# Sample attention of a decoder step: keys turned by VectorE, scores on small TensorE tiles, value products ahead of the filler

## The chip, the cores and the metric

The kernel runs on one core of a Trainium2 chip. The metric is the device time of one execution in microseconds (us); of the kernel before, three runs gave 3669.8, 3672.9 and 3675.2 us, median 3672.9.

## The reference, cut to what matters

One inference step of a hybrid decoder layer, for a prompt group (1024 tokens) and a sample group (8 sequences of 8 tokens). The change concerns the sample group's forgetting attention over a paged cache:

```python
k_all = jnp.concatenate([past_k, fk], axis=1)        # 4096 cached tokens (32 pages of 128) + 8 new
v_all = jnp.concatenate([past_v, fv], axis=1)
c_all = lax.cumsum(lf_all, axis=1)                   # log forget gates
s = jnp.einsum('bqhd,bkhd->bhqk', qi, k) * scale     # 8 heads of 64
s = s + ci[..., None] - ckT                          # bias c_t - c_s
p = jax.nn.softmax(s, axis=-1)
o = jnp.einsum('bhqk,bkhd->bqhd', p, v)
```

Everything is float32. Each page holds 128 tokens x 512 numbers (8 heads x 64), 256 KB for keys and as much for values; 256 pages are read of each.

## The kernel before, in words

The program is a row of phases with a barrier of all engines between them. Two of them are touched.

`phase_sample_bias` gathers the pages' forget gates, turns them on TensorE, adds them up over pages on VectorE (`tot`), and makes each page's bias with 16 pairs of matmuls, `own` (L2207) and `behind` (L2208), two halves of 8 pairs, whose stationary operand is 128 columns wide (16 pages x 8 heads). ScalarE copies each half out of PSUM (L2220), SyncE stores it to `bias_past` in DRAM (L2167). GpSimd also lays the queries out in `qz`.

`phase_sample` walks 8 sequences in 9 steps each: step 0 the 8 new tokens, steps 1 to 8 a quad of 4 pages. It goes on with the third gate of the merge, `w_fox_o` and the gate's weights, as filler: per sequence one block j of 128 channels. Every engine has its order written out in a loop over k = 0 to 75. TensorE's, in iteration k:

- `turn(u, 0)`, `turn(u, 1)` (L2488): 4 transposes of 128x128 for each of the first two pages of the quad that step k+1 needs, into PSUM (`ktp`, two buffers); ScalarE's `place` (L2629) copies each to `kt`.
- `turn_probs(k-1)` (L2501): 2 transposes of the exponentials, copied by VectorE's `place` (L2699) to `pt`.
- `fill(k)`: one piece of filler. Of a block's 9 pieces, 0, 1, 3, 4 are 12 gate matmuls of 512 columns (L2564), 2 and 5 are the output product (L2575), 6 is 24 gate matmuls of 64 columns; 7 and 8 are empty.
- `turn(u, 2)`, `turn(u, 3)`.
- `scores(k)` (L2516): 8 float32 products, `qz` stationary (128 rows x 32 columns, one of four column groups), 256 keys each. A float32 product is two instructions.
- `products(k-1)` (L2533): 8 products, `pt` stationary (32 columns), 256 value columns each.

Score rows of the same head and query stand in two column groups, one for even and one for odd pages, and are joined at the sequence's end (`swap_stats`, `pair_weights`, `finish`). VectorE adds the bias and takes the running minimum (`top`, L2717), ScalarE takes exponentials (`exps`, L2640), VectorE accumulates (L2728). `stp`, `ptp` and `ov` have two buffers.

SyncE issues all page loads: 4 key pages as their slots are turned, then 4 value pages once `valued` frees theirs (L2415, L2418); there is room for two quads of each. GpSimd issues bias loads (L2437) and the filler's weights (L2443, L2459) and splits these in high and low parts.

Of the kernel before, what the change touches and what calls it, by code (L numbers as in the profile page):

```python
# [13 lines left out]
F32 = mybir.dt.float32  # L14
# [42 lines left out]
def shape_tables():  # L57
# [19 lines left out]
    def dec(steps):  # L77
# [22 lines left out]
    set_of, row_of = i // 32, i % 32  # L100
    new_mask = np.tile(new.transpose(2, 1, 0), (P // LSEQ, 1, 1))
    new_mask[set_of % 2 == 1] = NEG
    swap = (i[None, :] == (i ^ 32)[:, None])
    comb = ((set_of // 2 * 32 + row_of)[:, None] == j[None, :])
# [4 lines left out]
        "new_mask": new_mask, "swap": swap, "comb": comb,  # L109
# [154 lines left out]
def phase_load(g):  # L264
# [3 lines left out]
    with ExitStack() as ctx:  # L268
# [8 lines left out]
        n_const = 8  # L277
        xs = io["x_sample"].rearrange("b t d -> (b t) d")
        with nc.Block() as block:
            @block.sync  # L280
            def _(sp):
# [21 lines left out]
                for e in range(2):  # L303
                    half = g.pages[:].rearrange("o (b n e) -> o b n e", b=NSEQ, e=2)[:, :, :, e]
                    sp.dma_start(half, io["page_table"][:, e * (NPG // 2):(e + 1) * (NPG // 2)].unsqueeze(0),
                                 allow_slow_non_contiguous=True).then_inc(consts, 16)
# [1828 lines left out]
def phase_sample_bias(g, qz, bias_n, bias_past):  # L2135
# [5 lines left out]
    with ExitStack() as ctx:  # L2141
# [5 lines left out]
        mask, lfx = g.sb(ctx, "d_mask", [P, NSEQ, TS]), g.sb(ctx, "d_lfx", [TS, 2, 2, 4, LSEQ])  # L2147
        out = g.sb(ctx, "d_out", [P, 2 * NSEQ, P])
        t = [g.ps(ctx, f"d_t{j}", [P, H_F, P]) for j in range(2)]
        sums = g.ps(ctx, "d_sums", [P, NSEQ, P])  # L2150
# [3 lines left out]
        expanded, cn_ok, qz_ok = g.sem("d_expanded"), g.sem("d_cn_ok"), g.sem("d_qz_ok")  # L2154
        indexed = g.sem("d_indexed")
        with nc.Block() as block:
            @block.sync
            def _(sp):
# [5 lines left out]
                for x in range(2):  # L2164
                    sp.wait_ge(read, x + 1)
                    for c in range(x * NSEQ, (x + 1) * NSEQ):
                        sp.dma_start(bias_past[c].rearrange("h g t -> g h t"), out[:, c, :]).then_inc(stored, 16)  # L2167
# [3 lines left out]
            def _(pool):  # L2171
# [6 lines left out]
                nc.gpsimd.memset(qz[:], 0.0).then_inc(qz_ok, 1)  # L2178
                pool.wait_ge(qz_ok, 1)
                pool.wait_ge(paged, 32)  # L2180
                for i in range(2):
                    q = g.br[:, 8 + i:12:2, TP:T].rearrange("p a (b q) -> p b a q", q=LSEQ)
                    for s in range(2):
                        at = 2 * LSEQ * i + LSEQ * s
                        nc.gpsimd.tensor_copy(qz[HALVES[s], :, i:PAIRS:2, at:at + LSEQ], q[HALVES[s]])

            @block.tensor
            def _(pe):
# [8 lines left out]
                nc.tensor.matmul(cn[:], lfx[:].rearrange("p a e s q -> p (a e s q)"), upto[:], start=True, stop=True)\  # L2197
                    .then_inc(cn_ok, 1)
                pe.wait_ge(copied, 2)
                pe.wait_ge(steps, 6)  # L2200
                for c in range(2 * NSEQ):
# [3 lines left out]
                    own = lft[:, b, x * HG:(x + 1) * HG, :].rearrange("p g h -> p (g h)")  # L2205
                    behind = tot[1][:, b, x * HG + 1:(x + 1) * HG + 1, :].rearrange("p g h -> p (g h)")
                    nc.tensor.matmul(sums[:, c % NSEQ, :], own, after[:], start=True, stop=False)  # L2207
                    mm = nc.tensor.matmul(sums[:, c % NSEQ, :], behind, g.ones[:], start=False, stop=True)  # L2208
# [4 lines left out]
            def _(act):  # L2213
                for j in range(2):
                    act.wait_ge(turned, j + 1)
                    nc.scalar.copy(lft[:, j * 4:j * 4 + 4].rearrange("p b g h -> p h (b g)"), t[j][:])\
                        .then_inc(copied, 1)
                for x in range(2):
                    act.wait_ge(summed, x + 1)
                    nc.scalar.copy(out[:, x * NSEQ:(x + 1) * NSEQ, :], sums[:]).then_inc(read, 1)  # L2220

            @block.vector
            def _(dve):
                chain = Chain(steps)
                nc.vector.memset(lfx[:], 0.0).then_inc(expanded, 1)
                for s in range(2):
                    nc.vector.memset(tot[s][:, :, NPG, :], 0.0)
                dve.wait_ge(expanded, 1)
                nc.vector.tensor_copy(lfx[:, :, 0], g.lfn[0:TS, NCH, :].rearrange("p (a s) -> p a s", s=4).unsqueeze(3)
                                      .broadcast_to([TS, 2, 4, LSEQ])).then_inc(expanded, 1)  # L2230
# [13 lines left out]
                assert now == 1 and chain.n == 6  # L2244
# [5 lines left out]
def phase_mix_two(g, mix):  # L2250
# [3 lines left out]
    with ExitStack() as ctx:  # L2254
# [72 lines left out]
        w.n = [b[0] + KD, b[1] + KD]  # L2327


def phase_sample(g, qz, bias_n, bias_past, mix):  # L2330

# [687 lines left out]
```

## Time and profile before

| | us |
|---|---|
| median of 3 runs | 3672.9 |
| profiled execution | 3673.46 |
| its span, first to last instruction | 3671.6 |
| PE busy / DVE / ACT / POOL | 3314.7 / 888.4 / 625.5 / 794.6 |
[...]

The span is the trace's; the execution's own time lies 1.9 us above it. PE is TensorE's matmuls, PEld its weight loads, DVE is VectorE, ACT ScalarE, POOL GpSimd, SP SyncE. Busy shares are means over very different stages, so one reads the two touched stages by themselves. They lie, in the trace, at about 1716 to 1768 us (bias) and 2091 to 2616 us (sample attention).

### The profile page before, as it was taken

The page shows a single profiled execution, that of the slowest core. Times are in us where ns is not written, and L with a number is a line of the kernel's source. Part 1 is how long each engine was busy: PE and PEld are TensorE (multiplying, and loading weights), DVE is VectorE, ACT ScalarE, POOL GpSimd, SP SyncE. Part 2 cuts the span into 40 slices and gives each one's busy share as a digit, 9 for nine tenths or more (in the row PEclk, how much of TensorE's full clock was granted, in tenths as well). Part 3 has the DMA queues.
Part 4 walks back from the last instruction along what each step waited for, and adds up shares of the span by engine and source line. Part 5 has one row for each costly group of instructions (what it writes and reads, how often), then busy time and mean ns, then how long its engine had stood idle before and what let it go on. Part 6 is the DMA issues. An engine that isn't in the chain of part 4 may idle for free. (4 is left out here: it accounts for less than half of the span.)

```text
span 3671.6 us, 56105 instructions
## 1 busy us (share of the span) xinstructions
PE 3314.7 (90%) x21121; PEld 2999.5 (82%) x21121; DVE 888.4 (24%) x1581; ACT 625.5 (17%) x1163; POOL 794.6 (22%) x696
## 2 busy tenths in 40 slices
PE   5999999997988898786799899999796999999996
PEld 5999999996887798554688666666686999999995
DVE  2111111114206211555101022222314111111114
ACT  3000000002101100344000144434203000000003
POOL 0232222323120131022111111111021223233220
PEclk8999999998997899899899999999798999999998
DMA  5111111111110112210211299999311111111111
GB/s 141 35 51 40 42 49 34 49 49 29 29 44 22 41 40 67 91 48 17 52 43 43 60 297 307 300 305 303 121 29 29 34 46 50 33 51 43 37 37 55
DMA packets 328667, 293.12 MB, mean 80 GB/s; under 512 B 33640, under 2 KB 249064, under 8 KB 328048
## 3 DMA queue, kind: packets, MB, share of 16 engines
q1 hardware_dynamic: 317136, 275.93, 24.3%
q0 software_dynamic: 11424, 15.76, 1.6%
q8 instruction: 68, 1.11, 0.1%
q14 instruction: 39, 0.32, 0.0%
HBM read 279.34 MB, written 12.26 MB: 79 GB/s over the span
## 5 line engine op out<-in xcount | busy, mean ns | idle before, releaser
L207 PE MATMUL f_acc<-x_hi,w_hi_last 128*128 128x364 f32 x1056 | 233.5, 329 | 27.5 <-SPq L489 27.5
L165 POOL CAST w_hi_first<-w_raw_first 128x1024 fp32r<-128x1024 f32 (+1 forms) x96 | 82.9, 863 | 738.4 <-issue 301.3
L207 PE MATMUL f_acc<-x_hi,w_hi_first 128*128 128x364 f32 x1056 | 233.5, 329 | 6.9 <-SPq L489 6.9
L207 PE MATMUL f_acc<-x_lo,w_hi_last 128*128 128x364 f32 x1056 | 234.0, 330 | 0.0
L207 PE MATMUL f_acc<-x_hi,w_lo_last 128*128 128x364 f32 x1056 | 234.0, 330 | 0.0
L207 PE MATMUL f_acc<-x_hi,w_lo_first 128*128 128x364 f32 x1056 | 233.9, 330 | 0.0
L207 PE MATMUL f_acc<-x_lo,w_hi_first 128*128 128x364 f32 x1056 | 233.7, 329 | 0.0
L207 PEld LDWEIGHTS f_acc<-x_hi,w_hi_last 128*128 128x128 f32 x1056 | 184.0, 189 | 28.0 <-issue 28.0
L165 POOL CAST w_hi_last<-w_raw_last 128x1024 fp32r<-128x1024 f32 (+2 forms) x92 | 73.5, 799 | 614.2 <-PE f_acc L207 610.2
L596 DVE SCALAR_TENSOR_TENSOR br<-f_acc,br 128x1092 f32 x88 | 114.1, 1296 | 368.8 <-PE f_acc L207 368.8
L207 PEld LDWEIGHTS f_acc<-x_hi,w_hi_first 128*128 128x128 f32 x1056 | 184.0, 189 | 7.1 <-issue 7.1
L167 POOL TENSOR_TENSOR w_lo_first<-w_raw_first,w_hi_first 128x1024 fp32r<-128x1024 f32 (+1 forms) x96 | 185.5, 1933 | 7.7
L207 PEld LDWEIGHTS f_acc<-x_hi,w_lo_last 128*128 128x128 f32 x1056 | 184.4, 189 | 0.0
L207 PEld LDWEIGHTS f_acc<-x_hi,w_lo_first 128*128 128x128 f32 x1056 | 184.2, 189 | 0.0
L207 PEld LDWEIGHTS f_acc<-x_lo,w_hi_last 128*128 128x128 f32 x1056 | 183.8, 189 | 0.0
L207 PEld LDWEIGHTS f_acc<-x_lo,w_hi_first 128*128 128x128 f32 x1056 | 183.7, 189 | 0.0
L2488 PEld LDWEIGHTS d_ktp<-ident_sb,br 128*128 128x128 f32 x1024 | 115.7, 143 | 83.1 <-DMA br<-cache_fox_k 45.5
L2488 PE MATMUL d_ktp<-ident_sb,br 128*128 128x128 f32 x1024 | 145.3, 283 | 34.8 <-DMA br<-cache_fox_k 32.7
L167 POOL TENSOR_TENSOR w_lo_last<-w_raw_last,w_hi_last 128x1024 fp32r<-128x1024 f32 (+2 forms) x92 | 162.9, 1771 | 7.4
L583 DVE TENSOR_TENSOR br<-br,f_acc 128x1092 f32<-128x1092 f32 x22 | 28.4, 1293 | 452.1 <-PE f_acc L207 452.1
L583 DVE TENSOR_TENSOR hid<-silu,f_acc 128x1092 f32<-128x1092 f32 x22 | 28.4, 1292 | 452.2 <-PE f_acc L207 452.2
L207 PE MATMUL f_acc<-h_hi,w_hi_last 128*128 128x364 f32 x528 | 118.0, 332 | 2.6 <-DVE h_lo L587 2.6
(399 smaller groups left out, 6321.8 us busy)
## 6 DMA issues: line engine op xcount, KB each, us to landing
br<-cache_fox_k SPq DMA_DIRECT2D x256, 256.0 KB, 5.6
br<-cache_fox_v SPq DMA_DIRECT2D x256, 256.0 KB, 6.5
w_raw_first<-w_ffn_gate SPq DMA_DIRECT2D x22, 512.0 KB, 3.8
w_raw_first<-w_ffn_up SPq DMA_DIRECT2D x22, 512.0 KB, 3.8
w_raw_last<-w_ffn_gate SPq DMA_DIRECT2D x22, 512.0 KB, 3.8
w_raw_last<-w_ffn_up SPq DMA_DIRECT2D x22, 512.0 KB, 3.8
w_raw_first<-w_ffn_down SPq DMA_DIRECT2D x40, 256.0 KB, 2.9
w_raw_last<-w_ffn_down SPq DMA_DIRECT2D x40, 256.0 KB, 2.8
```

Of the source, the lines that this page charges most:

```text
L165: self.nc.gpsimd.tensor_copy(hi, raw).then_inc(self.high[s], 1)
L167: self.nc.gpsimd.tensor_tensor(lo, raw, hi.bitcast(F32), ALU.subtract).then_inc(self.low[s], 1)
L207: mm = self.nc.tensor.matmul(out[:, b, 0:width], w[s][:, k, :], x[:, k, b * width:(b + 1) * width], start=(k == 0 and first), stop=(k == k ...
L583: nc.vector.tensor_tensor(blocks_of(hid), blocks_of(silu), acc[1][:, :, 0:TB], ALU.mult).then_inc(free[1], 1)
L596: nc.vector.scalar_tensor_tensor(blocks_of(row), acc[s][:, :, 0:TB], 0.5, blocks_of(row), ALU.mult, ALU.add).then_inc(free[s], 1)
L2488: mm = nc.tensor.transpose(ktp[n % 2][:, c, :], k_in[:, s, c * P:(c + 1) * P], g.ident[:])
```

## The change

- **Keys.** TensorE's 16 transposes per quad and ScalarE's 4 copies go. VectorE turns the quad in two instructions of 128 x 1024 numbers, which transpose each 32x32 block by itself (`turn`), after `top(k)` and ahead of `accumulate(k-1)`.
- **Scores.** 64 float32 products per quad (128 instructions), each on one 32x32 tile of the array: 32 rows, 32 stationary columns, 128 moving columns. Four row groups write to four PSUM banks. `stp` has one buffer. ScalarE replicates the queries for this (`queries`, two small copies per step).
- **Probabilities.** 512 per row and step instead of 256: 4 transposes, copied by ScalarE (`place`); one buffer each of `ptp`, `pt`, `ov`. All pages of a head share a row, so the joining at the end goes.
- **Products.** 16 of 128 value columns instead of 8 of 256.
- **Order of TensorE:** scores(k), turn_probs(k-1), products(k-1), turn_out, fill(k).
- **Filler.** Three blocks of 364 columns instead of 512, 512 and 64; all 9 pieces are filled.
- **Bias phase.** The 16 pairs of matmuls become 64 pairs with a stationary operand 32 columns wide (4 pages x 8 heads), and VectorE and ScalarE make 4 copies each to lay out `behind` and `own`. The layout of `qz` leaves this phase. Its 16 stores have 32 rows of 2 KB each.
- **Page table.** One load instead of two at the program's start.

```diff
@@ phase_sample_bias, TensorE @@
-                    nc.tensor.matmul(sums[:, c % NSEQ, :], own, after[:], start=True, stop=False)
-                    mm = nc.tensor.matmul(sums[:, c % NSEQ, :], behind, g.ones[:], start=False, stop=True)
+                    group, pages = slice(ROWS * (c % 4), ROWS * (c % 4 + 1)), slice(x * QUAD, (x + 1) * QUAD)
+                    for n in range(QUAD):
+                        at = by_token[group, c // 4 % 2, n]
+                        nc.tensor.matmul(at, own[:, b, n, pages, :]..., after[:], start=True, stop=False, ...)
+                        mm = nc.tensor.matmul(at, behind[:, b, n, pages, :]..., g.ones[:], start=False, stop=True, ...)
@@ phase_sample_bias, VectorE @@
+                for n in range(QUAD):
+                    nc.vector.tensor_copy(behind[:, :, n], tot[1][:, :, n + 1:NPG + 1:QUAD]).then_inc(behind_ok, 1)
@@ phase_sample, SyncE @@
+                        sp.wait_ge(k_turned, c * 4 + (2 * half + 2))
                         for s in range(half * QUAD, (half + 1) * QUAD):
-                            sp.wait_ge(k_turned, c * CH + (s + 1))
-                            sp.dma_start(k_in[:, s, :], keys[ahead[s]]...).then_inc(k_ok[s], 16)
+                            load_key(s, ahead[s])
@@ phase_sample, TensorE: scores @@
+                    pe.wait_ge(k_turned, 2 * (u + 1))
+                    for s in range(2):
+                        for h in range(2):
+                            for x in range(4):
+                                rows = slice(ROWS * x, ROWS * (x + 1))
+                                for c in range(PAIRS):
+                                    block = 4 * c + 2 * s + h
+                                    q = q_rep[e][rows, block * QW - s * LSEQ:block * QW - s * LSEQ + ROWS]
+                                    mm = nc.tensor.matmul(out[ROWS * c:ROWS * (c + 1), x], q,
+                                                          kt[u % 2][rows, :, block * ROWS:(block + 1) * ROWS],
+                                                          start=(s == 0 and h == 0), stop=(s == 1 and h == 1), ...)
+                    mm.then_inc(scored, 1)
@@ phase_sample, TensorE: order of an iteration @@
                 for k in range(STEPS_ALL + 4):
-                    u = quad_after(k)
-                    if u is not None:
-                        turn(u, 0)
-                        turn(u, 1)
+                    if k < STEPS_ALL:
+                        scores(k)
                     if 0 < k <= STEPS_ALL:
                         turn_probs(k - 1)
...
-                    fill(k)
-                    if u is not None:
-                        turn(u, 2)
-                        turn(u, 3)
-                    if k < STEPS_ALL:
-                        scores(k)
                     if 0 < k <= STEPS_ALL:
                         products(k - 1)
+                    if k >= PIECES + 1 and (k - 1) % PIECES == 0:
+                        turn_out((k - 1) // PIECES - 1)
+                    fill(k)
@@ phase_sample, ScalarE: an iteration @@
+                    if 0 < k <= STEPS_ALL:
+                        place(k - 1)
                     gate_read(k)
+                    if k + PIECES < STEPS_ALL:
+                        queries(k // PIECES + 1, k % PIECES)
                     if k < STEPS_ALL:
                         exps(k)
@@ phase_sample, VectorE @@
+                def turn(u):
+                    for s in range(u % 2 * QUAD, (u % 2 + 1) * QUAD):
+                        dve.wait_ge(k_ok[s], 16 * (u // 2 + 1))
+                    if u >= 2:
+                        dve.wait_ge(scored, step_of(u - 2) + 1)
+                    for y in range(2):
+                        nc.vector.transpose(kt[u % 2][:, 2 * y:2 * y + 2, :], k_in[:, u % 2, 2 * y:2 * y + 2, :])\
+                            .then_inc(k_turned, 1)
```

## Rows read from the trace of the kernel before

**Rows 1.** Windows, sample stage: length, busy us of each engine, PEclk, DMA share, GB/s.
```profile
2100.00:2591.00 491.00, 459.88 (x4087) 314.84 (x4087) 133.31 (x406) 205.18 (x498) 79.36 (x111) 0.97 0.92 300
```
**Rows 2.** Groups of the sample stage: shape, count, busy us, mean ns, idle before.
```profile
L2488 PE MATMUL d_ktp<-ident_sb,br 128*128 128x128 f32 x1024 | 145.3, 283 | 34.8 <-DMA br<-cache_fox_k 32.7 <-ACT mem_kt L2629 1.0
...
L2629 ACT COPY d_kt<-d_ktp 128x512 f32<-128x512 f32 x128 | 69.9, 587 | 78.6 <-PE d_ktp L2488 77.4
...
L2575 PE MATMUL fx_out<-br,fx_wo 128*128 128x512 f32 x128 | 57.6, 592 | 0.0
...
L2717 DVE CUSTOM_DVE_ANT_0 d_ring<-d_stp,d_ring,d_nm 128x256 f32<-128x256 f32 x64 | 31.0, 484 | 181.7 <-PE d_stp L2516 181.7
...
L2666 ACT ACTIVATE br<-fx_gate,br 128x512 f32<-128x512 f32 x16 | 11.0, 688 | 43.6 <-PE fx_gate L2564 43.6
```
**Rows 3.** Timeline of one step with a gate piece: start, us, instruction, count.
```profile
2567.67 1.10 PE L2488 MATMUL d_ktp<-ident_sb,br 128*128 128x128 f32 x8
...
2568.61 0.38 PE L2501 MATMUL d_ptp<-ident_sb,d_ring 128*128 128x128 f32 x2
...
2569.03 0.43 DVE L2699 COPY d_pt<-d_ptp 128x256 f32<-128x256 f32 x1 [0.59 <-PE d_ptp L2501]
...
2571.62 1.04 PE L2488 MATMUL d_ktp<-ident_sb,br 128*128 128x128 f32 x8
...
2572.60 0.40 PE L2516 MATMUL d_stp<-mem_v,d_qz 128*32 128x256 f32 x1
2572.61 0.40 PE L2516 MATMUL d_stp<-mem_kt,d_qz 128*32 128x256 f32 x1
...
2573.48 1.05 PE L2533 MATMUL d_ov<-br,d_pt 128*32 128x256 f32 x16
...
2574.46 1.09 PE L2488 MATMUL d_ktp<-ident_sb,br 128*128 128x128 f32 x8
```
**Rows 4.** Waits in the sample stage: us in total, times, longest.
```profile
PEld d_ktp L2488 <- DMA br<-cache_fox_k: 45.5, 34, 12.9
...
PEld d_ov L2533 <- DMA br<-cache_fox_v: 12.9, 22, 1.7
```
**Rows 5.** Windows of 2 us in the sample stage.
```profile
2442.00:2444.00 2.00, 2.00 (x6) 0.90 (x5) 0.00 (x0) 0.00 (x0) 0.00 (x0) 1.00 1.05 402
...
2446.00:2448.00 2.00, 2.00 (x32) 1.33 (x25) 0.97 (x3) 0.98 (x4) 0.00 (x0) 1.00 0.33 119
...
2488.00:2490.00 2.00, 2.00 (x18) 1.56 (x17) 0.00 (x0) 0.36 (x1) 0.00 (x0) 1.00 1.07 257
```
**Rows 6.** Timeline of the bias phase's sums.
```profile
1748.10 0.77 PE L2207 MATMUL d_sums<-d_after,d_lft 128*128 128x128 f32 x2 [14.45 <-DVE d_tot L2241]
...
1754.44 1.01 ACT L2220 COPY d_out<-d_sums 128x1024 f32<-128x1024 f32 x1 [18.70 <-PE d_sums L2208]
...
1755.84 0.39 PE L2208 MATMUL d_sums<-ones_sb,d_tot 128*128 128x128 f32 x2
...
1758.96 0.39 PE L2208 MATMUL d_sums<-ones_sb,d_tot 128*128 128x128 f32 x2
1759.38 1.01 ACT L2220 COPY d_out<-d_sums 128x1024 f32<-128x1024 f32 x1 [3.93 <-PE d_sums L2208]
```
**Rows 7.** Windows, bias phase and the retention phase's sample part.
```profile
1155.00:1170.00 15.00, 13.47 (x56) 12.21 (x56) 7.27 (x24) 0.00 (x0) 0.00 (x0) 0.50 0.22 52
...
1750.00:1752.00 2.00, 2.00 (x11) 2.00 (x11) 0.00 (x0) 0.00 (x0) 0.00 (x0) 0.50 0.00 0
...
1756.00:1758.00 2.00, 2.00 (x20) 2.00 (x20) 0.00 (x0) 0.00 (x0) 0.00 (x0) 1.00 0.27 66
```
**Rows 8.** VectorE's groups of 1024 and 512 numbers from SBUF to SBUF.
```profile
L2238 DVE TENSOR_TENSOR d_tot<-d_tot 128x1024 f32<-128x1024 f32 x1 | 1.2, 1226 | 0.0
...
L2241 DVE COPY d_tot<-d_tot 128x512 f32<-128x512 f32 x1 | 0.4, 420 | 0.0
```
**Rows 9.** Windows, first feed-forward phase, all matmuls of 364 columns.
```profile
200.00:300.00 100.00, 100.00 (x601) 100.00 (x600) 14.57 (x10) 5.70 (x6) 31.19 (x22) 1.00 0.17 49
```

More of the change, by code:

```diff
@@ L302, in _ @@
                 sp.dma_start(g.b_forget[:], io["b_forget"].rearrange("(h o) -> h o", o=1)).then_inc(consts, 16)
[L303 to L306, printed above, removed]
+                sp.dma_start(g.pages[:], io["page_table"].rearrange("b n -> (b n)").unsqueeze(0)).then_inc(consts, 16)
                 sp.wait_ge(consts, 16 * n_const)
@@ L2217, in _ @@
                         .then_inc(copied, 1)
+                act.wait_ge(copied, 2)
+                for n in range(QUAD):
+                    nc.scalar.copy(own[:, :, n], lft[:, :, n:NPG:QUAD]).then_inc(own_ok, 1)
                 for x in range(2):
                     act.wait_ge(summed, x + 1)
-                    nc.scalar.copy(out[:, x * NSEQ:(x + 1) * NSEQ, :], sums[:]).then_inc(read, 1)
+                    nc.scalar.copy(out[:, x * 2:(x + 1) * 2, :], sums[:]).then_inc(read, 1)
             @block.vector
@@ L2467, in _ @@
-                weights(0)
+                for e in range(2):
+                    nc.gpsimd.memset(q_rep[e][:], 0.0).then_inc(zeroed, 1)
+                    nc.gpsimd.memset(qz[e][:], 0.0).then_inc(zeroed, 1)
                 bias(0)
-                split(0)
                 bias(1)
+                raw_half(0, 0)
+                out_weights(0)
+                split_half(0, 0)
+                raw_half(0, 1)
                 for b in range(NSEQ):
-                    more = b + 1 < NSEQ
-                    if more:
-                        bias(2 * b + 2)
-                        weights(b + 1)
-                        split(b + 1)
-                        bias(2 * b + 3)
+                    split_half(b, 1)
+                    bias(4 * b + 2)
+                    bias(4 * b + 3)
+                    if b + 1 < NSEQ:
+                        bias(4 * b + 4)
+                        raw_half(b + 1, 0)
+                        bias(4 * b + 5)
+                        out_weights(b + 1)
+                        split_half(b + 1, 0)
+                        raw_half(b + 1, 1)
@@ L2498, in turn_probs @@
                     else:
-                        half, m = divmod(b * (PIECES - 1) + v - 1, QUAD)
-                        for x in range(2):
-                            mm = nc.tensor.transpose(ptp[:, k % 2, x, :], ring[half % 2][:, m, x, :], g.ident[:])
+                        for y in range(QUAD):
+                            mm = nc.tensor.transpose(ptp[:, y, :], probs[:, y, :], g.ident[:])
                     mm.then_inc(pturned, 1)
@@ new lines, in scores @@
+                    if k > 0:
+                        pe.wait_ge(topped, k)
+                    if k >= PIECES + 2 and v == 2:
+                        pe.wait_ge(out_ok, b)
+                    if v == 0:
+                        pe.wait_ge(q_ok, 18 * (b + 1))
+                        for c in range(PAIRS):
+                            mm = nc.tensor.matmul(stp[ROWS * c:ROWS * (c + 1), 0, 0:TS], qz[e][:, c, :], g.k_s[:, c, :],
+                                                  start=True, stop=True)
+                        mm.then_inc(scored, 1)
+                        return
@@ L2521, in products @@
+                    mm.then_inc(scored, 1)
                 def products(k):
@@ L2560, in gate_part @@
+                    nc.tensor.transpose(ot, on[:], g.ident[:]).then_inc(ot_ok, 1)
+                def gate_part(j, x, ks):
+                    if ks[0] == 0 and 4 * j + x > 0:
+                        pe.wait_ge(gated, 4 * j + x)
                     if x == 0:
```

434 lines of the change are left out of this document (193 added, 241 removed).

## The prediction, made before the change was timed

> **What bounds the kernel now.** I read the windows first: the change touches the sample stage and the bias phase, so only these count. In the 491 us in which pages stream, TensorE is busy 459.9 us and the DMA engines 0.92 of the time [rows 1]. Neither is the bound alone. The waits say the same from the other side: TensorE's weight loads wait 45.5 us for keys (12.9 of them for the first page) and 12.9 us for values [rows 4]. The 2 us windows show why: the DMA share stands at 1.05 with 402 GB/s, falls to 0.33 while TensorE works through a long step with all buffers full, and is 1.07 again at only 257 GB/s when GpSimd's loads run beside the pages [rows 5]. So full use reads as about 1.05, and the two resources limit each other in turn.
>
> Per sequence (a batch of 9 steps) the stage takes 491/8 = 61.4 us. **DMA alone:** 0.92 x 61.4 / 1.05 = 53.8 us. **TensorE alone:** a step with a gate piece repeats in 2574.46 - 2567.67 = 6.79 us: 8 key transposes 0.83, 2 of probabilities 0.22, 12 gate matmuls 2.79 (from 2568.83 to 2571.62, so 0.2325 each), 8 transposes with the drain 0.98, 16 score instructions 0.88, 16 of products 0.86, the rest 0.12 for changing the array's shape [rows 3]. With an output piece (8 x 0.45 = 3.6 instead of 2.79 [rows 2]) 7.6; with 24 short gate matmuls at 0.11, 6.6; without filler 4.0. Four, two, one and two of these, less 3.0 for what the step of new tokens lacks, plus 0.8 for swap and output: 4 x 6.79 + 2 x 7.6 + 6.6 + 8.0 - 2.2 = 54.8 us. The two floors are 53.8 and 54.8 and the batch takes 61.4: about 7 us is lost in alternation.
>
> **The change: the sample stage.** *Scores.* The trace shows no 32x32 tiles. Four tiles of different columns start together (2572.60, 2572.61) and 16 instructions of 256 columns end 0.88 us later, so four run abreast at 0.22 each [rows 3]; 128 columns take half. If 16 tiles run abreast, 8 rounds of 0.11 are 0.89 us; issuing 16 pairs per round costs about the same, and I take 1.0. If only the four column groups do, 128 / 4 x 0.11 = 3.5 us. I take 1.0, since columns demonstrably overlap and the row groups have separate banks; 3.5 stays the other end.
>
> [...]
>
> *Probabilities.* Now nothing stands between transposes and products but ScalarE's copy. From the first transpose to the copy 0.42 us with two, so 0.64 with four [rows 3]; a copy of 128x512 from PSUM 0.59 [rows 2]; handing over 0.06: 1.29 us, of which 0.85 is idle. *Products:* 32 instructions of half the length, 0.86 as before. *Filler:* 364 columns go at 100/601 = 0.166 us [rows 9], 12 are 2.0; the output pieces keep their columns. A batch has 6 x 2.0 + 2 x 2.4 + 2.0 = 18.8 us. *Shape changes:* three or four of 0.12 and a drain of 0.15. [...]
>
> A step without filler is then 1.0 + 1.29 + 0.86 + 0.4 = 3.55 us, the one of new tokens about 1.8. Three times per batch the exponentials stand behind the gate's tanh (0.69 at 512 columns [rows 2], some 0.55 at 364) and two small query copies, and turn_probs waits 0.9 more. Batch: 8 x 3.55 + 1.8 + 18.8 + 2.7 + 0.4 = 52.1 us, against 54.8. The key transposes' 145.3 us of PE [rows 2] are mostly spent again: on the idle time at the copy, two more transposes and the wait for the exponentials.
>
> *VectorE.* Not shown in the trace: a block transpose of 1024 numbers. Nearest is 1.23 us for 1024 [rows 8]; bounds 0.69 (a copy at the rate of 420 ns for 512, scaled with its fixed part) and 2.5. I take 1.2, 2.4 for the pair. Before it stands `top`: 0.48 for 256 [rows 2], so 0.83 to 0.9 for 512. Scores at 0, top ends at 2.1, turn at 4.5, well before the next scores at 5.6; only at 2.5 us an instruction would it set the step (about 7 us). Queued behind a turn that waits for its pages are accumulate and add_mix; products of the next step need the first, a step later, so the wait is covered.
>
> *DMA.* The bytes stay. Keys for two quads ahead are now issued four at once as the turn ends, values once the quad before last is multiplied, which the new order does ahead of the filler. Bias loads come in 4 smaller portions per batch. Steps are more equal (no empty filler pieces, no 7.6 us ones), so of the 7 us lost I expect half back: batch = 53.8 + 3.8 = 57.6, **8 x 3.8 = -30 us**. Bounds: nothing lost, 53.8, -61 us; nothing gained, 0; scores four abreast, 8 x 2.5 = 20 more on TensorE, 72.5, +89 us. The stage's ends (less to load at the start, one filler piece more behind the last product, no joining) I put at 0 +-3. Page table and GpSimd's query layout lie beside other work: 0.
>
> **The bias phase** is on the path: barriers stand around it and nothing runs beside its matmuls. Before, 64 instructions: those of the second half start 28 in 1758.96 - 1755.84 = 3.12 us, 0.111 each; the first half, 32 in 6.3 us, ran mostly at half clock [rows 6, 7]. After, 256 instructions of the same 128 moving columns, 16 in a row on the same column group, so not abreast: 192 more x 0.111 = 21.3, less one overlap at each of 16 changes of group, 1.7: 19.6 us. VectorE's four strided copies of 512, 0.42 to 0.69 each [rows 8, 2], stand behind the last sum: 2.2. ScalarE's four lie beside VectorE's additions: 0. **+22 us.** If column groups did overlap, +2 at least for the copies; that would need another order of the loop, and I give it little.
>
> **Sum.** 3673.5 (the profiled execution) - 30 + 22 = 3665.5; the median of the runs is 0.6 below it, so 3665.
>
> **The rivals.**
> 1. *The clock stays low in the bias phase.* [...] In the retention phase it stays at 0.50 with TensorE busy 13.5 of 15 us [rows 7], so busy alone doesn't lift it, and a quarter of the columns may not either. Then 256 x 0.213 = 54.5 against 9.6: +45 with the copies; total -30 + 47 = +17, 3690. Against it: the stream has no gaps.
> 2. *The small score tiles don't run 16 abreast,* by rows or by issue. From about 1.0 us more per step TensorE's batch passes 61.4 and it decides; at 3.5 us the stage costs 89 more: about 3785. For: no row tile in the trace. Against: the four columns.
> 3. *DMA was the bound all along*, and a batch stays within 1 us of 61.4: -5 + 22 = +17, 3690. For: 0.92. Against: the windows at 0.33.
> 4. *The stage reaches its floors:* 55 us, -50 + 22: 3645.
>
> **How the numbers follow.** Forecast 0.50, rivals 0.13, 0.10, 0.14 and 0.13. The likeliest case's own range is 3648 to 3682. Below 3632 and above 3704 I leave 0.06 and 0.12. A measurement of this kernel tells 0.2%, 7.3 us, from no change. The forecast, -8, is split 0.30 faster, 0.15 same, 0.05 slower; rival 4 adds 0.13 to faster; rivals 1, 2 and 3 add 0.10, 0.10 and 0.11 to slower and 0.06 to same. Faster 0.43, same 0.21, slower 0.36.
>
> **What would show it.** Score instructions of a quad spanning 1.0 us (3.5: rival 2). A gap of about 0.85 us ahead of each quad's products. VectorE's turns near 1.2 us. DMA share in the stage up from 0.92 to about 0.98, the stage some 30 us shorter. The bias phase's sums 30 us instead of 11.3 from first to last, at granted 1.00 after the first 5. I am wrong if products wait for values in most steps, if the clock falls in the stage because of the new idle time, or if the bias phase costs nothing.

## The result, and the profile after

The changed kernel takes 3776.4 us (median of 4 runs, 3770.1 to 3790.2) against 3674.1 beside it: ratio 1.0285, 95% interval [1.0255, 1.0316]. It is 102 us slower; forecast were 9 us less, with 3704 as the upper end. The profiled execution is the slowest of the four (3790.2 us, span 3788.2), 14 us above the median, so what is read from its trace is somewhat larger than the 102.

The sample stage first, from the first scores of keys to the last, in windows (columns as in [rows 1]; that row is the one of before):

```profile
2126.00:2326.00 200.00, 161.17 (x3997) 117.92 (x3986) 83.92 (x143) 51.01 (x154) 38.41 (x59) 0.85 0.85 260
2326.00:2526.00 200.00, 156.67 (x3756) 117.52 (x3754) 82.32 (x151) 51.15 (x156) 42.57 (x65) 0.87 0.81 243
2526.00:2709.00 183.00, 144.09 (x3546) 108.50 (x3547) 76.40 (x132) 42.09 (x125) 32.22 (x50) 0.88 0.85 259
```

583 us where before took 491. TensorE is busy 461.9 us, as before, but in 2.8 times as many matmul instructions and with the granted clock down from 0.97 to 0.87; DMA fell from 0.92 to 0.84. Neither resource is full. One marker gives the length of a batch of nine steps without its ends: the normalised result of each sequence (start of the first to start of the last of eight). Before, then after:

```profile
L2758 DVE TENSOR_SCALAR d_on<-d_acc,d_pair_w,d_total x8: 411/413/501, 2172.8 to 2599.0; 128x256 f32<-128x256 f32 x8
```
```profile
L2754 DVE TENSOR_SCALAR d_on<-d_acc,d_total x8: 286/286/291, 2199.5 to 2717.9; 128x128 f32<-128x128 f32 x8
```

(2599.0 - 2172.8)/7 = 60.9 us and 74.1 us. Of the 116.6 us by which the spans differ, 92.2 lie in these seven batches, 26.7 ahead of the first marker (16 in the bias phase, the rest mainly in the first batch), and -2.3 behind the last. In these seven batches TensorE was busy 397.7 us before and is busy 410.4 now; its idle time went from 28.3 to 107.6 us. So most of the loss is idle time.

What TensorE's matmuls wait for in the stage (us in all, times, longest):

```profile
PE d_ov L2545 <- ACT d_pt L2656: 43.2, 68, 0.7
PE d_stp L2527 <- issue: 25.7, 16, 4.7
PE d_ov L2545 <- issue: 21.1, 12, 3.9
PE d_ov L2545 <- DMA br<-cache_fox_v: 17.5, 25, 2.7
...
PE fx_out L2574 <- issue: 4.8, 2, 3.1
PE fx_gate L2562 <- issue: 2.8, 2, 2.1
```

The first row is the forecast gap at the copy, 0.6 to 0.7 us a quad. The "issue" rows are new: 54.4 us in 32 gaps in which TensorE waits for nothing that the profile shows. The old kernel has none in its stage. The rows list gaps; they are not yet time that the kernel would gain without them. One step shows the rest (start, us, instruction, idle before it):

```profile
2305.68 1.64 PEld L2527 LDWEIGHTS d_stp<-d_kt,d_q_rep 32*32 32x32 f32 x128 [0.51 <-issue]
2305.69 1.90 PE L2527 MATMUL d_stp<-d_kt,d_q_rep 32*32 32x128 f32 x128
...
2308.30 2.37 DVE L2701 STREAM_TRANSPOSE d_kt<-br 128x1024 f32<-128x1024 f32 x2
...
2308.85 0.42 PE L2545 MATMUL d_ov<-br,d_pt 128*32 128x128 f32 x8 [0.68 <-ACT d_pt L2656]
2309.14 2.66 SPq L2425 DMA_DIRECT2D br<-cache_fox_v  x4
...
2309.70 0.43 PE L2545 MATMUL d_ov<-br,d_pt 128*32 128x128 f32 x8 [0.42 <-DMA br<-cache_fox_v]
...
2311.90 0.85 PE L2545 MATMUL d_ov<-br,d_pt 128*32 128x128 f32 x9 [1.07 <-issue]
```

128 scores take 1.64 us of weight loads in every quad at full clock (granted 1.00), 12.8 ns for a load and its matmul; the gap ahead of the products; values that come page by page; and, within one set of products, a gap of 1.07 us that nothing in the profile explains. The gate matmuls behind it start 0.30 us apart (2313.15, 2313.45, 2313.75), not 0.166: the granted clock is 0.50 there.

The queue that brings instructions, of the whole page, after (before: 68 packets, 1.11 MB):

```profile
q8 instruction: 126, 2.06, 0.2%
```

2.06 MB in 126 packets is 16 KB a packet, and 0.95 MB for 70641 - 56105 = 14536 instructions more is 65 bytes each. By that estimate a packet is some 250 instructions, and the scores of one quad, 128 loads and 128 matmuls, use up one in 1.64 us. That these packets come too late is the theory that the experiments test; no row shows a packet being waited for.

The bias phase, sums of the changed kernel (windows):

```profile
1755.00:1760.00 5.00, 5.00 (x46) 4.47 (x45) 0.00 (x0) 0.00 (x0) 0.00 (x0) 0.69 0.00 0
...
1768.00:1779.00 11.00, 11.00 (x128) 10.86 (x126) 0.00 (x0) 0.00 (x0) 0.00 (x0) 1.00 0.14 50
```

11.0/128 = 0.086 us is a mean of two things. Start, us, instruction, at full clock (the rows between, of weight loads, left out):

```profile
1758.98 0.38 PE L2198 MATMUL d_sums<-d_after,d_own 128*32 128x128 f32 x2
...
1759.20 0.38 PE L2200 MATMUL d_sums<-ones_sb,d_behind 128*32 128x128 f32 x2
...
1759.41 0.41 PE L2198 MATMUL d_sums<-d_after,d_own 128*32 128x128 f32 x4
...
1759.63 0.41 PE L2200 MATMUL d_sums<-ones_sb,d_behind 128*32 128x128 f32 x4
```

Within a column group two instructions take 0.22 us, 0.11 each, as before. Where the group changes, four take the same 0.22 to 0.25: the last four of one group run beside the first four of the next, and 16 take 1.35 us (1759.41 to 1760.76) instead of 1.76. In all the sums take 26.2 us from first to last where [rows 6] shows 11.3, and the four copies 1.43. Together +16.3.

### The profile page after: what moved, and what is told of

Same layout as the page of the kernel before. It is cut to its first block and busy times, and to the rows that moved or that the text cites. A ratio compares the mean times of both kernels' runs of the same rounds, so it can differ in the third digit from the quotient of the medians.

```text
span 3788.2 us, 70641 instructions
## 1 busy us (share of the span) xinstructions
PE 3334.0 (88%) x28569; PEld 3043.5 (80%) x28569; DVE 1000.9 (26%) x1601; ACT 572.6 (15%) x1127; POOL 825.9 (22%) x759
## 3 DMA queue, kind: packets, MB, share of 16 engines
q8 instruction: 126, 2.06, 0.2%
## 5 line engine op out<-in xcount | busy, mean ns | idle before, releaser
L2527 PE MATMUL d_stp<-d_kt,d_q_rep 32*32 32x128 f32 x8192 | 131.9, 285 | 39.2 <-issue 25.7
L2545 PE MATMUL d_ov<-br,d_pt 128*32 128x128 f32 x2048 | 91.2, 309 | 79.1 <-ACT d_pt L2656 40.5
L2527 PEld LDWEIGHTS d_stp<-d_kt,d_q_rep 32*32 32x32 f32 x8192 | 101.8, 105 | 72.5 <-issue 65.4
L2701 DVE STREAM_TRANSPOSE d_kt<-br 128x1024 f32<-128x1024 f32 x128 | 151.5, 1222 | 6.7 <-DMA br<-cache_fox_k 6.3
```

What stands on the lines that cost most here:

```text
L2527: mm = nc.tensor.matmul(out[ROWS * c:ROWS * (c + 1), x], q, kt[u % 2][rows, :, block * ROWS:(block + 1) * ROWS], start=(s == 0 and h == 0) ...
L2545: mm = nc.tensor.matmul(ov[ROWS * c:ROWS * (c + 1), :], pt[0:P if v else TS, y, ROWS * c:ROWS * (c + 1)], values, start=(y == 0), stop=(y ...
L2701: nc.vector.transpose(kt[u % 2][:, 2 * y:2 * y + 2, :], k_in[:, u % 2, 2 * y:2 * y + 2, :])\
```

## The experiments

Theory at the start: TensorE runs out of delivered instructions, because the loads fill the DMA engines that also bring its code. Rivals: the price of the small tiles themselves, late loads, the gap at the copy, the clock. All results, each beside runs of before on its chip (medians 3671.7 to 3673.9); batch is the marker's distance:

| kernel | us | ratio [95%] | batch |
|---|---|---|---|
| few | 3746.7 | 1.0203 [1.0186, 1.022] | 69.6 |
| after_small | 3702.9 | 1.0084 [1.0068, 1.0101] | 63.4 |
| before_small | 3662.6 | 0.9972 [0.9961, 0.9983] | 60.3 |
| before_pieces | 3710.2 | 1.0103 [1.0086, 1.012] | 65.8 |
| fill_first | 3752.7 | 1.0226 [1.02, 1.0252] | 69.3 |
| few_values_first | 3702.3 | 1.0079 [1.0054, 1.0105] | 64.7 |
| bias_abreast | 3763.7 | 1.0243 [1.0222, 1.0263] | |
| before_blocks | 3678.3 | 1.0019 [1.0007, 1.0031] | 62.5 |
| before_unrolled | 3635.1 | 0.9892 [0.9875, 0.9908] | 56.7 |
| after_unrolled | 3760.8 | 1.0237 [1.022, 1.0254] | 70.2 |
| after_best | 3730.9 | 1.0153 [1.0136, 1.017] | 69.4 |
| few_best | 3671.8 | 0.9993 [0.9984, 1.0003] | 61.6 |
| before_twice | 3650.2 | 0.9938 [0.9917, 0.9959] | 58.7 |
| before_small_unrolled | 3624.7 | 0.9867 [0.9849, 0.9886] | 55.9 |
| after_small_best | 3621.3 | 0.9852 [0.9831, 0.9872] | 56.1 |
| before_unrolled_blocks | 3643.9 | 0.9917 [0.9892, 0.9942] | 58.9 |

### few: a quarter of the score matmuls

```diff
-for x in range(4):                       # four row groups, 128 instructions a quad
-    rows = slice(ROWS * x, ROWS * (x + 1))
-    ... matmul(out[ROWS*c:ROWS*(c+1), x], q[rows], kt[rows, :, block])
+... matmul(out[ROWS*c:ROWS*(c+1), 2*s + h], q, kt[:, :, block])    # 32 a quad
```

> The changed kernel with a quad's scores in 32 instructions instead of 128: 16 products of all 128 rows on a column group (each fills one bank), which stream the same 8 rounds of 128 columns; the four row groups' tokens are summed together, so the scores are wrong sums. The trace of the changed kernel shows TensorE idle for nothing the profile can name ('issue') for 54 us in the sample stage, in gaps of 1 to 5 us some 20 us apart, and 91 instruction-queue packets there against 34 before. Theory supply (TensorE runs out of fetched instructions): the gaps go nearly all, 50 us and more faster than the changed kernel, and with the shorter issue (below) about 3776 - 50 - 40 = 3685 or less. Theory small tiles (only the tiles' own rate of 1.64 us per quad instead of 0.9 is dear, the gaps have another cause): 64 x 0.75 = 48 us faster, 3728, gaps still there. Theory clock (TensorE's idle time at the probabilities keeps it at half clock for parts of the stage, mean 0.86): little faster than by the tiles, clock stays near 0.86.

-30, less than both expected. But the gaps are gone: no "issue" row on a matmul is left in the stage. Other waits took their place:

```profile
PE d_ov L2542 <- DMA br<-cache_fox_v: 60.6, 50, 5.0
PE d_ov L2542 <- ACT d_pt L2653: 37.9, 60, 0.7
```

So fewer instructions end the gaps, and values, late by 17.5 us before, are late by 60.6. This run changes two things, though: a quad's scores also get shorter, from 1.64 us of weight loads and 1.90 of matmuls to 0.81 and 1.08, 0.82 us for each of 64 quads, 52 us. Its seven batches:

```profile
2188.00:2675.00 487.00, 367.20 (x4601) 263.40 (x4601) 214.51 (x381) 128.96 (x388) 99.91 (x152) 0.87 0.89 267
```

TensorE is busy 43.2 us less than in the changed kernel (410.4), about what the shorter scores give, and idle 12.2 us more (119.8 against 107.6). The time gained is no more than the scores gave; TensorE's idle time only changed its name. The granted clock, 0.87, didn't rise either.

### after_small and before_small: both kernels with loads of 16 columns

```diff
-sp.dma_start(k_in[:, u, x], keys[page]...)          # 512 columns; the values alike
+sp.dma_start(k_in[:, u, x, 0:16], keys[page]...[:, 0:16])
```

> The changed kernel, but each page load brings only 64 bytes of each row instead of 2 KB (keys and values are mostly old data; the result is wrong), so the DMA engines are almost idle in the stage. Theory supply, in its form that instruction fetches starve behind page traffic: the gaps shrink to well under 15 us in all. If the fetch itself is too slow for 176 matmuls and as many weight loads per quad even on quiet queues, the gaps stay. Theory small tiles or TensorE's own order: TensorE's floor shows, about 6.3 us a step by the trace's undisturbed steps, so a stage of 8 x (8 x 6.3 + 4) = 435 us instead of 585, 3776 - 150 = 3626.

> The kernel before with the same small page loads (wrong data). It gives TensorE's floor of the old order: the prediction worked out 54.8 us per batch against 61.4, so 8 x 6.6 = 53 us faster than before, 3621. The changed kernel's floor was put at 52.1. If DMA alone had bound the old kernel it would be far less than that; if TensorE alone, the same as before.

The changed kernel gains 73 us, with the same instructions and the same 126 packets of code; its gaps fall from 54.4 to 10.2 us. So busy DMA engines make most of the gaps, not all: after_small_best, further down, still has 20.0 us of them with loads as small. Seven batches in windows, the changed kernel and then the one with small loads:

```profile
2200.00:2718.00 518.00, 410.44 (x9976) 308.13 (x9976) 214.48 (x381) 128.93 (x388) 99.90 (x152) 0.88 0.83 252
```
```profile
2186.00:2629.00 443.00, 371.86 (x9967) 281.79 (x9967) 214.06 (x380) 128.99 (x388) 99.97 (x152) 0.96 0.23 43
```

Of the 75 us, 38.6 are TensorE's busy time: the same matmuls at a granted 0.88 instead of 0.96. The other 36.4 are idle time. Theory supply's sign, gaps well under 15 us, is there; the time, 3703, is far from the 3626 of TensorE's own order.

The old kernel gains only 11. With loads of 3% of the bytes it was still 60.3 us a batch and waited 25.2 us for keys. So DMA did not bound it, and TensorE, at a forecast 54.8, didn't either. Something else paced it; that came out below.

### before_pieces: the old kernel with four times the score and product instructions

```diff
-matmul(stp[rows, k % 2, 0:n], qz, keys)               # 256 columns
+for part in range(4): matmul(stp[rows, k % 2, part*64:part*64+64], qz, keys_of(part))
```
The products are cut alike.

> The kernel before with each score product of 256 columns cut in four of 64 and each value product likewise: same result, same columns streamed in the same column groups, but 128 matmul instructions and as many weight loads per quad in place of 32. It gives the old order the new instruction load and nothing else. Theory supply: gaps without a releaser appear on TensorE in the stage, some 30 to 50 us, and the kernel is that much slower, about 3705 to 3725. Theory small tiles (a tile of 32 rows is what costs): at most the issue rate, 13 ns per pair of load and matmul, 128 x 0.013 = 1.65 against 1.72 us streamed: no change, 3674.

+36.7, as theory supply expected, and the gaps appear in the old kernel (six rows with "issue", 43.3 us in all; two of them):

```profile
PE d_ov L2539 <- issue: 28.3, 17, 3.7
...
PE d_ktp L2488 <- issue: 5.8, 3, 3.7
```

The work, its order and its loads are the old ones. In seven batches TensorE is idle 49.9 us instead of 28.3 and busy 410.1 instead of 397.7, at a granted 0.96 instead of 0.98; the waits for keys fall from 19.0 to 4.1 us in the stage. So here the gaps cost time, about half of it net of the waits that they replace. That the gaps hang on the number of instructions and on the loads is shown from three sides: count down, loads down, count up. That they are waits for packets of code is the reading that fits all three; no trace shows it directly. What they cost the changed kernel is another question, and stays open: in few, and in few_best below, TensorE has no less idle time without them.

### fill_first: the filler ahead of the products

```diff
 turn_probs(k - 1)
+fill(k)
 products(k - 1)
 ...
-fill(k)
```

> The changed kernel with TensorE's filler piece moved between the turn of the probabilities and the value products of each step. In the changed kernel's trace TensorE waits 43.2 us in the stage for ScalarE to place the turned probabilities and 17.5 us for values, 60.7 us in all, right ahead of the products; a piece of about 3 us covers both. Theory A (the order is a part of the loss, beside the supply of instructions): the 60.7 us go but for the ninth steps, some 45 to 60 us, and the granted clock rises with the idle time gone: 3710 to 3735. Theory B (the stage is as long as the supply of instructions or the loads make it, so that idle time only moves): 3765 to 3780, and the gaps that end with nothing the profile shows grow by what the others lose.

-24, between the two. The gap at the copy (43.2 us) is gone, values still wait 16.7, and the "issue" gaps grew from 54.4 to 75.6 us, by half of what the copy's gap had been. The granted clock of seven batches rose from 0.88 to 0.91, and most of what was gained there is busy time (24.9 us of 33), as theory A had the clock rise. Another 13.9 us are waits for the filler's weights, now needed earlier.

### few_values_first: values issued ahead of keys

```diff
+sp.wait_ge(valued, ...); four value loads of this quad
 sp.wait_ge(k_turned, ...); four key loads of the quad after next
-sp.wait_ge(valued, ...); four value loads of this quad
```

> The kernel with 32 in place of 128 score matmuls per quad (most of the sums of the scores left out), and in SyncE's loop the four value loads of a quad ahead of the four key loads of the quad after next. Without the swap (3746.7 us) TensorE waits 60.6 us for values; in its trace the value loads of a quad are issued at 2339.95, right behind the key loads that began at 2337.82 when the turn ended, while the values' own condition, the products two quads before, was met at about 2336. Theory A (issued late): the values come 2 to 4 us earlier in each of 64 steps and most of the 60.6 us go: 3690 to 3710. Theory B (the transfers themselves are full, DMA share 0.89 between 2300 and 2500): the wait moves from the values to the keys: 3740 to 3750.

-44.4 against few: the values were issued late. They had stood in SyncE's queue behind keys that wait for VectorE's turn and that are needed a step later. In the wait list values fall from 60.6 to 20.9, and turned keys rise from 11.6 to 44.3: a part of the wait moved, as theory B has it, but the smaller part.

### bias_abreast: four column groups in turn

```diff
-for c in range(8): for n in range(4): own(c, n); behind(c, n)
+for c0 in (0, 4): for n in range(4): for src in (own, behind): for c in range(c0, c0 + 4): src(c, n)
```

> The changed kernel with the loops of the bias sums turned inside out: four matmuls in a row go to four different groups of 32 columns of the array, instead of eight to the same. The 256 sums took 26.2 us in the changed kernel, 0.086 us for one at full clock. Theory A (matmuls in one column group follow one another, in four they overlap; the value products of a quad, 32 of 128 columns, take 1.08 us, 0.034 each): 256 x 0.034 = 9 us at full clock, some 12 with a start at half clock, so 14 us less: 3762. Theory B (the price is one of issuing a matmul): 3776, within 4 us.

-12.6, Theory A. The 256 sums now take 11 us, as long as the 64 before; at full clock eight start in 0.22 us, 0.027 each. So the order of the loop was the cost, not the count.

### before_blocks: the new filler alone

```diff
-cols = slice(x * 512, (x + 1) * 512) if x < 2 else slice(TP, T)      # 512, 512, 64
+cols = slice(x * TB, (x + 1) * TB)                                   # three of TB = 364
```

> The kernel before with the changed kernel's filler alone: three blocks of 364, 364 and 296 columns (the 64 of the sample in the third of the gate), nine pieces for nine steps, in place of two blocks of 512 and one of 64 in seven. From the rows of before a gate matmul of 512 columns starts 0.23 us after the last and one of 64 some 0.1; of 364 columns 0.166. One batch: 24 x 3 x 0.166 = 12.0 us in place of 24 x 2 x 0.23 + 24 x 0.1 = 13.4, and two steps that had no filler get one. Theory A (TensorE's own work and order bound the old stage): -12 to -20 us, 3655 to 3662. Theory B (the loads bound it, share 0.92): 3670 to 3676.

+5, outside both. The shorter pieces did what they should, but the filler now waits 20.8 us for the split weights of GpSimd, and nothing is gained. That fits a stage which TensorE did not pace; since the new waits could have eaten a gain, it doesn't show it.

### before_unrolled and before_twice: SyncE's loop

What was left to read was SyncE's queue. In the old kernel with small loads it shows this (start, us, count):

```profile
2186.21 0.91 SPq L2415 DMA_DIRECT2D br<-cache_fox_k  x2
2187.30 1.88 SPq L2418 DMA_DIRECT2D br<-cache_fox_v  x4
2195.25 2.09 SPq L2415 DMA_DIRECT2D br<-cache_fox_k  x4
2197.52 2.42 SPq L2418 DMA_DIRECT2D br<-cache_fox_v  x4
2200.19 2.06 SPq L2415 DMA_DIRECT2D br<-cache_fox_k  x4
2202.43 1.88 SPq L2418 DMA_DIRECT2D br<-cache_fox_v  x4
```

16 issues back to back (the first rows are the end of a chunk), then 6 us of nothing before the next chunk. The loop's head reads 16 page numbers into registers there.

```diff
-with sp.Fori(0, CHUNKS - 1) as c:
-    ahead, now = pages(c + 1), pages(c)       # 16 reads
+now = first
+for c in range(CHUNKS - 1):                   # written out
+    ahead = pages(c + 1)                      # 8 reads
     ...
+    now = ahead
```

(The expectation says 16 chunks; there are 32 of two quads, four to a batch.)

> The kernel before with SyncE's loop over the 16 chunks (two quads each) written out, so that the page numbers of a chunk are read into registers once (8 reads) and not twice (16). In the trace of before SyncE issues the 16 loads of a chunk back to back and then shows nothing for about 6 us before the next chunk: 2193.66 to 2199.73, 2208.94 to 2215.02, 2224.64 to 2230.71. With loads of 16 columns it is the same, 2189.18 to 2195.25, and the chunk there, 14.6 us, is filled by SyncE alone. Theory A (SyncE's loop is what paces the old stage): the pause halves at least, and the batch goes from 61.4 to what is next, the floors of DMA 53.8 and TensorE 54.8 with some loss, 57 to 58 us: 3640 to 3655. Theory B (TensorE's order paces it, the pause is slack): 3668 to 3676. Theory C (the pause is code being fetched, and longer code makes more of it): slower than before.

-38.7 us, 1.1%, a little more than expected: faster than both kernels, and the fastest here of those that leave nothing out. Before, SyncE waited 7.3 us in 490 for others, so it was hardly ever ahead. Now it waits for TensorE:

```profile
SPq L2416 <- PE d_ktp L2490: 48.7, 35, 3.1
SPq L2419 <- PE d_ov L2535: 34.2, 34, 1.3
```
The stage then runs near both floors at once; its window for seven batches:

```profile
2168.00:2564.00 396.00, 388.52 (x3584) 269.39 (x3576) 118.50 (x365) 175.60 (x432) 67.49 (x95) 0.98 0.98 324
```

> The kernel before with SyncE's loop over the chunks written out, but the page numbers of each chunk still read twice, 16 reads a chunk. With 8 reads it is 3635.1. Theory A (the pause of 6 us is made of the reads and of the arithmetic on what they give, some 0.37 us each): with 16 of them and no loop the pause is 5 to 6 us and the time 3660 to 3674. Theory B (the pause is the loop's branch and the fetch of its code): 3635 to 3640.

Neither theory: 3650.2. The pause is 5.4 to 5.7 us with 16 reads and no loop, 6.0 to 6.1 with the loop, and 2.8 in before_unrolled, with 8 reads and no loop. So the reads are most of it, 0.34 us each, with the index arithmetic that goes with a read (before_twice executes 55731 instructions, before_unrolled 54931: 800 more for 256 more reads, some three each). The loop's own 0.7 us or so in each of 32 chunks makes 22, and 21 were gained: up to here SyncE paced the stage, and what it lost per chunk was paid in full. The next 2.6 us a chunk, 83 in all, gave only some 15 more, since TensorE and the loads then hold it.

### after_unrolled, after_best and few_best: the changed kernel repaired

> The changed kernel with the same edit of SyncE's loop. The chunk there is 19 us with the same pause of 6 us, of which SyncE's waits for turned keys (97 us in the stage) take up the rest. Theory A (in the changed kernel the supply of TensorE's instructions and the place gap, 54 and 43 us of idle time, pace the stage): only the 17.5 us for late values go, 3755 to 3766. Theory B (SyncE's loop paces this stage too): 8 x 3 us and more, 3735 to 3750.

-16 as Theory A has it, though the waits for values only fall from 17.5 to 6.5 us. SyncE's loop did not pace this stage; SyncE waits 155 us for turned keys.

> The changed kernel with all four: bias sums four abreast, filler ahead of the products, value loads ahead of the key loads, SyncE's loop written out. Measured alone: the first 3763.7 (-13), the second 3752.7 (-24). Theory A (the supply of instructions remains: in the kernel with the filler ahead the gaps that end with nothing grew from 54.4 to 75.6 us): 3776 - 13 - 24 - 20 = 3720, within 10 us. Theory B (the gaps were slack behind the loads): under 3690.

> As the last, with 32 in place of 128 score matmuls per quad (most of the sums of the scores left out): what the changed kernel would be without its instruction count. With values first alone 3702.3; TensorE waits there 44.6 us for placed probabilities, 44.3 for turned keys, 20.9 for values. Theory A: the first two go with filler ahead and faster page reading, the bias sums give 13: 3630 to 3650, so that the count of TensorE's instructions decides by itself between slower and faster than before. Theory B (it is as slow as the variant with all matmuls): 3700 or more.

With all four repairs the changed kernel takes 3730.9, just outside the 3720 within 10 of Theory A. It is still 57 us slower than before and 96 slower than before_unrolled. Its gaps without a named wait are larger than ever:

```profile
PE d_stp L2529 <- issue: 52.2, 34, 4.9
...
PE d_ov L2547 <- issue: 14.8, 6, 4.3
PE fx_gate L2564 <- issue: 14.3, 6, 4.4
```

With a further row of 3.9 they make 85 us. With a quarter of the scores they are 0.6 us and the time is 59 us less. The shorter scores alone take 52 us (0.82 x 64, as in few) off TensorE's work, and its idle time does not fall: 99.4 us in seven batches with 85 us of gaps, 108.9 with none to speak of. How the 59 divide between the two isn't shown, since few_best runs into other waits. The window of few_best:

```profile
2166.00:2596.00 430.00, 321.14 (x4575) 255.43 (x4568) 216.33 (x377) 128.19 (x384) 99.84 (x152) 0.91 0.98 302
```

So the loss adds up: 3776.4 - 45.5 for the four repairs - 59.1 for the number of score matmuls = 3671.8, the time of before. But it isn't the 3630 to 3650 of Theory A. TensorE waits 55.5 us for turned keys and 27.3 for the filler's split weights, and few_best is at DMA share 0.98 with only 302 GB/s, where before_unrolled moves 324 at the same share. GpSimd's queue takes a larger part (13.7% of the engines against 11.1%, 16421 packets against 8352 in the 400 us from 2180): the new bias rows are loaded in smaller packets. That is a cost of the change which the bytes hid; it is read from the pages, not tested.

### before_small_unrolled and after_small_best: TensorE alone

> The kernel before with SyncE's loop written out and loads of 16 of the 512 columns of a page (the other columns of keys and values are left unloaded). With full loads it is 3635.1 with a batch of 56.7 us, DMA share 1.02. Theory A (DMA is what is next there, and TensorE right behind it at 54.8): 3620 to 3630. Theory B (TensorE alone holds it): 3633 to 3637.

> The changed kernel with loads of 16 columns, bias sums abreast, filler ahead of the products and SyncE's loop written out: TensorE's work alone. With small loads only it is 3702.9 with a batch of 63.4 us, of which TensorE waits 35.2 + 29.3 us in the stage for placed probabilities and values. Theory A (the scores at 1.64 us a quad, 0.64 over the predicted 1.0, so a floor of 52.1 + 8 x 0.64 = 57.2 us a batch): 3702.9 - 13 - 8 x (63.4 - 57.7) = 3644, within 8. Theory B (the predicted floor of 52.1 holds): about 3605.

The old kernel's 3624.7 is Theory A. The changed one's 3621.3 lies between its two theories (3644 and 3605). With loads and SyncE out of the way the two designs are equal, 55.9 and 56.1 us a batch, so as built the change neither costs nor brings anything on TensorE. They come to it differently: of these seven batches TensorE is busy 384.4 us in the old kernel and 352.9 in the changed one, which is idle for 40 us. In the stage 20.0 us of its waits are gaps without a named wait, in 17 pieces of up to 2.8 us, with the DMA share at 0.27.

### before_unrolled_blocks

> The kernel before with SyncE's loop written out (3635.1) and the changed kernel's filler of nine pieces. Alone the filler gave +5 (3678.3, with 20.8 us of waits for POOL's split weights, which come later there). Theory A (TensorE has now little to spare, so the 1.4 us per batch that the pieces save count): 3625 to 3632. Theory B (the waits for the weights stay, or DMA at 1.02 holds it): 3635 to 3645.

3643.9, Theory B: +8.8 over before_unrolled; 18.1 us of waits for the split weights.

## Why the prediction was wrong, point by point

- **What bounds the kernel.** This failed first. "The two resources limit each other in turn" with 7 us lost per batch: neither did. SyncE's issue loop paced the batch; the waits for keys [rows 4] and the swinging windows [rows 5] were its trace. The prediction did not read SyncE's queue. The old TensorE floor, 54.8, was right within 1.1 (55.9).
- **"Of the 7 us lost I expect half back", -30: the step that failed.** It takes the larger of two floors, DMA's 53.8, adds 3.8, and lets TensorE's 52.1 lie hidden beside it. Outside the bias phase the changed kernel lost 86 us by the medians (100 in the profiled execution) instead. A batch takes 74.1 us, with DMA at 0.83; TensorE is busy in 58.6 of them and idle in 15.4. Its work and its waits followed one another in each step and the loads did not cover them: 43 us less of busy time made few 30 us faster, and the four repairs and the fewer score matmuls together gave back all of it (few_best, 3671.8). Left out were the place of the value loads in SyncE's queue and the supply of instructions, a term put at nothing. Its gaps are shown (54 us); what they cost is shown in before_pieces (+36.7 with the finer cut), while in the changed kernel they mostly took the place of other waits.
- **The new TensorE batch of 52.1.** With loads nearly off and the order unchanged it is 63.4 (after_small). The term that was sized worst is *scores*, "issuing 16 pairs per round costs about the same, and I take 1.0". No row shows what issuing costs; "about the same" was the author's estimate. They took 1.64 us of loads and 1.90 of matmuls, the same in every step at full clock that goes through without a gap. Columns and rows do run side by side (far below the 3.5 of rival 2); what decides is 12.8 ns to issue a pair, which the prediction had named and not priced. The 32 larger matmuls of few and few_best take about the predicted 1.0, and the 0.82 us between makes 52 us in 64 quads, the largest single item of the loss.
- **The supply of instructions.** The old kernel has no gap without a named wait in its stage; the changed kernel has 32, 54.4 us in all, where a packet of 16 KB lasts 1.64 us in the scores beside a DMA share of 0.84.
- **Rival 2** came nearest to the number (3785), and that is luck: it has the scores at 3.5 us, and by its own rule ("from about 1.0 us more per step") the measured 0.64 to 0.90 would have changed nothing. Its words "or by issue" were right.
- **Gap at the copy, 0.85:** 0.67, a fifth less. **VectorE's turn, 1.2:** 1.222, right. **Copies behind the last sum, 2.2:** 1.43.
- **Values.** "Products wait for values in most steps" was named as what would make me wrong. They wait 25 times in 64 steps, 17.5 us. few_values_first shows, for the kernel with fewer scores, that the order in SyncE's loop holds them back.
- **The clock.** It fell in the stage, as feared: 0.97 to 0.87. It is half of the difference between loads on and off. In the step shown above it fell to 0.50 at about 2311 us, in the gap of 1.07 us; in the three us before, TensorE had been busy 0.33, 0.58 and 0.54 of each. It isn't the gaps at the supply alone: few has none and stands at 0.87 in its seven batches, the changed kernel at 0.88. That idle time is what lowers it is argued, not shown, since no run changes only that.
- **The bias phase, +22:** +16.3. Sign and mechanism right: within a group not abreast, and bias_abreast takes the price back. The 0.111 of one was right too (0.11). The term mis-sized is "less one overlap at each of 16 changes of group, 1.7": a change saved 0.41 us, not 0.11, and there are 14 inside the two halves. With the copies, 0.8 less than taken, that is most of the difference. Rival 1 fell: the sums begin at 1753.0 us at a granted 0.50, and the clock stands at 1.00 from 1759.
- **Slips in the sums.** None decides anything. The parts listed for a step of 6.79 us add up to 6.56, so the rest is 0.23, at two places, and not 0.12. That it is the price of changing the array's shape, and the 0.15 one of a drain, is the author's reading of such remainders; no run shows either by itself. Rival 2's batch is 52.1 + 20 = 72.1, not 72.5, and its stage +86. Rival 1's +45 is without the copies. No row shows the 2.5 us that bounds VectorE's turn from above; it took 1.22.

## What to carry to other kernels

Before crediting two nearly full resources with limiting each other, read the issuing queue: here 16 issues back to back, a pause of 6 us and 7.3 us of waits in 490 meant that the queue's own instructions set the pace. Price a change also in instructions: 128 small pairs of load and matmul took 0.82 us more than 32 larger ones with the same columns, and where a packet of code was used up in 1.6 us beside full page loads, TensorE stood still for up to 4.9 us at a time. A gap in a wait list is not yet time to be gained: take it away in a run and see whether TensorE's idle time falls or only changes its name. Order matmuls so that neighbours lie in different column groups (0.027 us each instead of 0.11 in bias_abreast), and issue first the load that is needed first (44.4 us in few_values_first).

## What the runs showed of the hardware that was not expected

- A read of a number into a register of SyncE, with its index arithmetic, costs 0.34 us (16 reads 5.4 in before_twice, 8 reads 2.8 in before_unrolled), and one issued load of a page 0.47 (1.88 for four, before_small).
- A 32x32 fp32 load and matmul are issued every 12.8 ns (after, 128 in 1.64 us); a 128x32 pair with 128 columns every 25 (few, 0.81 us for 32).
- Code comes in packets of 16 KB (after, 126 packets with 2.06 MB). TensorE has gaps without a named wait when it uses it up fast: 54.4 us in the stage beside full loads, 10.2 and 20.0 with loads of 3% of the bytes, none with a quarter of the scores.
- fp32 matmuls of 128 columns in one group of 32 columns follow one another at 0.11 us; in four groups in turn at 0.027 (bias_abreast).
